# Four chunks of a part worked as one run of high, then low products, in an fp32 decoder trunk on one core

## What is computed

```python
def reference(x, ...):
    h = x
    for i in range(2):
        xn = rms_norm(h, norm_mix[i])
        if i == 0:   # HGRN2: q, f, v, g = split(xn @ w_in (2048 x 8192)); gated recurrence over 16 heads
            mix = hgrn2_mixer(xn, ...)        # ... then rms_norm, * silu(g), @ w_out (2048 x 2048)
        else:        # B, C, h = split(xn @ w_in (2048 x 6144)); (B * conv3(C * h)) @ w_out
            mix = short_conv_mixer(xn, ...)
        h = h + mix
        xn = rms_norm(h, norm_ffn[i])         # gate, val = split(conv3(xn @ w_up (2048 x 11264)))
        h = h + (silu(gate) * val) @ w_down   # w_down: 5632 x 2048
    return rms_norm(h, final_norm)
```

## Time and profile before

| | us |
|---|---|
| median of 3 runs (2368.31 to 2370.46) | 2368.76 |
| the profiled execution's own time | 2369.03 |
| its span, first to last instruction | 2367.2 |
| PE busy | 2339.4 (99%) |
| PE weight loads busy | 2049.0 (87%) |
| DVE busy | 1708.5 (72%) |
| ACT busy | 1043.5 (44%) |
| DMA engines, mean share / rate | some 60% / 184 GB/s |

### The profile page before, as it was taken

The page is one execution under the profiler, slowest core; times in us unless marked ns, Lnnn a source line. Parts: engine busy times, 40 slices in busy tenths (PEclk is TensorE's granted clock), DMA queues, the critical chain, the costliest instruction groups (busy, mean ns, idle before and its releaser), DMA issues.

```text
span 2367.2 us, 36548 instructions
## 1 busy us (share of the span) xinstructions
PE 2339.4 (99%) x13219; PEld 2049.0 (87%) x13219; DVE 1708.5 (72%) x2153; ACT 1043.5 (44%) x1151; POOL 2.7 (0%) x8
## 2 busy tenths in 40 slices
PE   7999999999999999999999999999999999999998
PEld 6888888888888888888888888888888888888886
DVE  6878788878878878865555666667788788785443
ACT  6443434454444444444444444444444444443443
POOL 0000000000000000000000000000000000000000
PEclk9999999999999999999999999999999999999999
DMA  6555555466666665655556656556656666665664
GB/s 197 169 179 160 166 160 164 152 192 188 186 194 185 187 194 179 194 190 187 188 185 192 188 187 187 187 188 186 194 180 192 189 184 188 193 202 185 193 193 144
DMA packets 411833, 434.90 MB, mean 184 GB/s; under 512 B 13344, under 2 KB 387040, under 8 KB 411616
## 3 DMA queue, kind: packets, MB, share of 16 engines
q1 hardware_dynamic: 411264, 432.51, 59.2%
q10 hardware_dynamic: 480, 1.18, 0.1%
HBM read 431.54 MB, written 2.10 MB: 183 GB/s over the span
## 4 chain that ended last, share of the span: by engine, by line
PE 96%; DVE 1%; issue 1%; ACT 1%; DMA 0%; SPq 0%; ACTq 0%; DVEq 0%
PE acc L1050 54%; PE acc L1056 28%; PE acc L1085 3%; PE acc L1086 3%; PE acc L1084 3%; PE acc L1068 2%; PE side L1179 1%; PE acc L1070 1%; PE side L1151 0%; DMA raw<-in_hgrn_w_in 0%; PE side L1174 0%; ACT w_parts L336 0%; DVE kl L788 0%; DVE a_diag L825 0%; DVE a_diag L819 0%
## 5 line engine op out<-in xcount | busy, mean ns | idle before, releaser
L545 DVE TENSOR_TENSOR w_parts<-raw,w_parts 128x1024 fp32r<-128x1024 f32 x816 | 994.4, 1223 | 578.9 <-ACT w_parts L336 569.0
L336 ACT ACTIVATE w_parts<-raw 128x1024 fp32r<-128x1024 f32 x816 | 862.6, 1060 | 1181.4 <-PE acc L1056 975.4
L1050 PE MATMUL acc<-xn,w_parts 128*128 128x512 f32 x4352 | 1094.5, 393 | 3.2 <-DVE xn L604 3.2
L1050 PEld LDWEIGHTS acc<-xn,w_parts 128*128 128x128 f32 x4352 | 783.7, 189 | 144.3 <-DVE xn L604 3.6
L1056 PEld LDWEIGHTS acc<-xn,w_parts 128*128 128x128 f32 x4352 | 594.1, 190 | 42.8
L1056 PE MATMUL acc<-xn,w_parts 128*128 128x256 f32 x4352 | 607.0, 282 | 0.0
L1050 PE MATMUL acc<-act,w_parts 128*128 128x512 f32 x1216 | 305.0, 393 | 1.6 <-DVE act L859 1.6
L1050 PEld LDWEIGHTS acc<-act,w_parts 128*128 128x128 f32 x1216 | 218.7, 189 | 41.0 <-DVE act L859 1.8
L1056 PEld LDWEIGHTS acc<-act,w_parts 128*128 128x128 f32 x1216 | 165.9, 190 | 11.9
L1056 PE MATMUL acc<-act,w_parts 128*128 128x256 f32 x1216 | 169.5, 282 | 0.0
L1084 PE MATMUL acc<-w_parts,act 128*128 128x512 f32 x352 | 137.3, 390 | 0.0
(11 more groups left out here) (131 smaller groups left out, 1005.2 us busy)
## 6 DMA issues: line engine op xcount, KB each, us to landing
raw<-in_ffn_w_up SPq DMA_DIRECT2D x352, 512.0 KB, 4.1
raw<-in_ffn_w_down SPq DMA_DIRECT2D x176, 512.0 KB, 4.3
raw<-in_hgrn_w_in SPq DMA_DIRECT2D x128, 512.0 KB, 3.6
raw<-in_sc_w_in SPq DMA_DIRECT2D x96, 512.0 KB, 4.5
raw<-in_hgrn_w_out SPq DMA_DIRECT2D x32, 512.0 KB, 3.6
raw<-in_sc_w_out SPq DMA_DIRECT2D x32, 512.0 KB, 4.6
x_tok<-in_x SPq DMA_DIRECT2D x4, 512.0 KB, 8.0
out<-h SPq DMA_DIRECT2D x4, 512.0 KB, 4.1
```

The costliest lines, as they stand in the source:

```text
L336: nc.scalar.activation(w_parts[:, c % RING, :, 0, :], raw[:, c % RING], ACT.Copy).then_inc(hi_ready, 1)
L545: v.tensor_tensor(w_parts[:, c % RING, :, 1, :], raw[:, c % RING], w_parts[:, c % RING, :, 0, :].bitcast(F32), ALU.subtract).then_inc(lo_r ...
L1050: mm(to[:, j, :], w[:, q, 0, j * P:(j + 1) * P], src[:, k * KW + q, :, :].rearrange("p n t -> p (n t)"), start=begin and q == 0, stop=Fals ...
```

## The change

A group is worked in runs of chunks: 4 in UP0, UP1, SC_IN and SC_OUT, 2 in HGRN_IN, HGRN_OUT and DOWN0, 1 in DOWN1. PE does the high products (512 columns) of all chunks of a run, then the low products (256 columns) of all of them. `chunk_used` becomes two counts: `hi_used`, raised by the last high product of a chunk, which ACT's `split` waits for, and `lo_used`, raised by its last low product, which DVE's `split` now waits for beside `hi_ready`. In the value group of HGRN_IN the 512-column matmuls (both weight parts moving) of two chunks come first and free the low slots, then the 256-column ones free the high slots. What PE did after chunk kk of a run (stages, turns) now stands after the high products of the run, for the last chunk of the run after its low products. In `PLAN` levels 0 and 2 move one chunk later. The program of DOWN1 is as it was, but for the two counts.

```diff
+RUN = 2
...
-PLAN = [(2, LEVEL, -1), (3, LEVEL, 0), (5, LEVEL, 1), (6, LEVEL, 2), (8, LEVEL, 3), (10, LEVEL, 4),
+PLAN = [(2, LEVEL, -1), (4, LEVEL, 0), (5, LEVEL, 1), (7, LEVEL, 2), (8, LEVEL, 3), (10, LEVEL, 4),
         (12, LEVEL, 5), (13, LEVEL, 6), (15, LEVEL, 7), (18, OUTPUT, 0)]
...
-        chunk_used = sem("chunk_used")
+        hi_used = sem("hi_used")
+        lo_used = sem("lo_used")
...
                 act_e.wait_ge(w_loaded[c % RING], at(i, 4 * phase.cpi, 16 * (c // RING + 1)))
-                act_e.wait_ge(chunk_used, at(i, phase.cpi, c + 1))
+                act_e.wait_ge(hi_used, at(i, phase.cpi, c + 1))
                 nc.scalar.activation(w_parts[:, c % RING, :, 0, :], raw[:, c % RING], ACT.Copy).then_inc(hi_ready, 1)
 
             def correction(i, phase, g, part, c):
 
-                act_e.wait_ge(chunk_used, at(i, phase.cpi, c + 1 + RING))
+                done = hi_used if phase is HGRN_IN and g == V_GROUP else lo_used
+                act_e.wait_ge(done, at(i, phase.cpi, c + 1 + RING))
                 a = g * phase.parts + part
                 act_e.wait_ge(acc_free, at(i, phase.api, phase.a0 + a + SETS))
...
                 dve.wait_ge(hi_ready, at(i, phase.cpi, c + 1))
+                dve.wait_ge(lo_used, at(i, phase.cpi, c + 1))
                 v.tensor_tensor(w_parts[:, c % RING, :, 1, :], raw[:, c % RING],
                                 w_parts[:, c % RING, :, 0, :].bitcast(F32), ALU.subtract).then_inc(lo_ready, 1)
...
-                        dve.wait_ge(chunk_used, at(i, phase.cpi, c + 1 + RING))
+                        dve.wait_ge(lo_used, at(i, phase.cpi, c + 1 + RING))
...
-            def features(to, c, src, k, begin, end, await_low):
+            def feature_highs(to, c, src, k, begin):
 
                 w = w_parts[:, c % RING]
                 for q in range(KW):
                     for j in range(TW):
-
-                        mm(to[:, j, :], w[:, q, 0, j * P:(j + 1) * P],
-                           src[:, k * KW + q, :, :].rearrange("p n t -> p (n t)"), start=begin and q == 0, stop=False,
-                           skip_group_check=True)
-                await_low()
+                        o = mm(to[:, j, :], w[:, q, 0, j * P:(j + 1) * P],
+                               src[:, k * KW + q, :, :].rearrange("p n t -> p (n t)"), start=begin and q == 0,
+                               stop=False, skip_group_check=True)
+                o.then_inc(hi_used, 1)
+            def feature_lows(to, c, src, k, end):
+                w = w_parts[:, c % RING]
                 for q in range(KW):
                     for j in range(TW):
                         o = mm(to[:, j, T:], w[:, q, 1, j * P:(j + 1) * P], src[:, k * KW + q, 0, :], start=False,
                                stop=end and q == KW - 1, skip_group_check=True)
-                return o
-
-            def tokens(to, c, src, k, begin, end, await_low):
+                o.then_inc(lo_used, 1)
+            def x_block(src, t, n, b):
+                return x_mirror[:, t, n] if b else src[:, t, n, 0:P]
+            def token_boths(to, c, src, k, begin):
 
                 w = w_parts[:, c % RING]
-                await_low()
                 for q in range(KW):
-                    t = k * KW + q
                     for b in range(T // P):
-                        x_hi, x_lo = ((x_mirror[:, t, n] if b else src[:, t, n, 0:P]) for n in range(2))
-                        mm(to[:, b, :], x_hi, w[:, q].rearrange("p n d -> p (n d)"), start=begin and q == 0, stop=False,
-                           skip_group_check=True)
-                        o = mm(to[:, b, T:], x_lo, w[:, q, 0, :], start=False, stop=end and q == KW - 1,
-                               skip_group_check=True)
-                return o
-
...
-                        for kk, (part, k, begin, end) in enumerate(phase.steps(first, g)):
-                            c = phase.c0 + g * phase.cpg + kk
-                            a = g * phase.parts + part
-                            if begin:
-
-                                pe.wait_ge(acc_free, at(i, phase.api, phase.a0 + a + 1))
-                            need = k + 1 if phase.parts == 2 else k * KC // TG + 1
-                            if first and g == 0 and need > seen:
-                                pe.wait_ge(ready, ready0 + need * per)
-                                seen = need
-
-                            def await_low():
-                                pe.wait_ge(lo_ready, at(i, phase.cpi, c + 1 + RING))
-
-                            pe.wait_ge(hi_ready, at(i, phase.cpi, c + 1))
-                            work = features
-                            if first and phase is HGRN_IN and g == V_GROUP and part == 0:
-                                pe.wait_ge(mirror_ready, k + 1)
+                        steps = phase.steps(first, g)
+                        run = 1 if phase is DOWN1 else 2 * RUN if phase in (UP0, SC_IN, SC_OUT, UP1) else RUN
+                        for k0 in range(0, phase.cpg, run):
+                            chunks = []
+                            for kk in range(k0, k0 + run):
+                                part, k, begin, end = steps[kk]
+                                c = phase.c0 + g * phase.cpg + kk
+                                a = g * phase.parts + part
+                                if begin:
+                                    pe.wait_ge(acc_free, at(i, phase.api, phase.a0 + a + 1))
+                                need = k + 1 if phase.parts == 2 else k * KC // TG + 1
+                                if first and g == 0 and need > seen:
+                                    pe.wait_ge(ready, ready0 + need * per)
+                                    seen = need
+                                pe.wait_ge(hi_ready, at(i, phase.cpi, c + 1))
+                                to = acc[:, a % SETS]
+                                if phase is DOWN1:
+                                    pe.wait_ge(lo_ready, at(i, phase.cpi, c + 1 + RING))
+                                    wide_tokens(to, c, src, k, begin, end)
+                                elif phase is HGRN_IN and g == V_GROUP:
+                                    if first and part == 0:
+                                        pe.wait_ge(mirror_ready, k + 1)
+                                    pe.wait_ge(lo_ready, at(i, phase.cpi, c + 1 + RING))
+                                    token_boths(to, c, src, k, begin)
+                                else:
+                                    feature_highs(to, c, src, k, begin)
+                                chunks.append((c, to, k, end))
                             if phase is DOWN1:
-                                work = wide_tokens
-                            elif phase is HGRN_IN and g == V_GROUP:
-                                work = tokens
-                            work(acc[:, a % SETS], c, src, k, begin, end, await_low).then_inc(chunk_used, 1)
-                            if carry and first:
-                                carry(g, kk)
-                            if first and rs and (g, kk) == rs_at:
-                                sum_squares(*rs)
-                            if pieces:
-                                pieces(i, first, g, kk)
+                                between(i, first, g, k0)
+                                continue
+                            for kk in range(k0, k0 + run - 1):
+                                between(i, first, g, kk)
+                            for c, to, k, end in chunks:
+                                if phase is HGRN_IN and g == V_GROUP:
+                                    token_highs(to, c, src, k, end)
+                                else:
+                                    pe.wait_ge(lo_ready, at(i, phase.cpi, c + 1 + RING))
+                                    feature_lows(to, c, src, k, end)
+                            between(i, first, g, k0 + run - 1)
...
-            pe.sem_inc(chunk_used, RING)
+            pe.sem_inc(hi_used, RING)
+            pe.sem_inc(lo_used, RING)
```

More of the change, by code:

```diff
@@ L475, in final @@
                 if first and (g, kk) == (0, 0):
-                    act_e.wait_ge(chunk_used, DOWN1.c0 + RING)
+                    act_e.wait_ge(lo_used, DOWN1.c0 + RING)
                     act_e.dma_start(final_w[:], final_norm.partition_broadcast(P)).then_inc(final_w_loaded, 16)
@@ L983, in final @@
                     return
-                dve.wait_ge(chunk_used, DOWN1.c0 + (n + 1) * DOWN1.cpg + RING)
+                dve.wait_ge(hi_used, DOWN1.c0 + (n + 1) * DOWN1.cpg + RING)
                 for b in range(T // P):
@@ L1057, in features, with token_highs, wide_tokens @@
                                stop=end and q == KW - 1, skip_group_check=True)
-                return o
-            def tokens(to, c, src, k, begin, end, await_low):
+                o.then_inc(lo_used, 1)
+            def x_block(src, t, n, b):
```

(39 more changed lines are left out.)

## The result

The changed kernel takes 2424.92 us (median of 4 runs, 2423.79 to 2426.68), the kernel before 2369.59 in the runs beside it: a ratio of 1.0233, 95% interval 1.022 to 1.0246. It is 55 us slower. The forecast was 40 us slower (2409.5, range 2380 to 2432), so the direction and the kind of loss came out, and the size some 15 us short.

What follows compares the result with a forecast made beforehand. PE's matmul stream was taken to bound the kernel. The terms, -9 + 32 + 10 + 4 + 2.5 + 1 = 40.5 us, on the profiled 2369.0 gave 2409.5 us, range 2380 to 2432.

Steps and rivals of the forecast that it cites:

- A: All regrouped phases: fewer turns between high and low products save 9 us, bounds 0 and -12.
- the rival of a full overlap: Long runs let weight loads overlap fully, matmuls fall to columns over 2.4 GHz: -108 us, 2310 in all; chance 4%.
- The rule that the prediction took from the Trainium skill: Matmul gap set by columns alone, 216 ns for 512; order worth nothing, waits stay: 2418 us, chance 12%.
- B: UP0 and UP1: PE waits 1.44 us for the last chunk's high split, 22 times: +32 us, bounds 20 to 42.
- C: HGRN_IN's value group, four iterations: +2.2 us each for level 1, +0.3 for later levels: +10, bounds 2 and 18.
- D: HGRN_OUT's first group: PE's wait for the last tile of `act` grows to 5.9 us: +4, bounds 2 and 6.
- E: Kernel start: less work ahead of the wait for input tile 2, next tile later: +2.5 us, bounds 0.5 and 4.
- F: Other phase starts, where DVE's last work of a phase holds a bank: +1 us, bounds 0 and 3.
- That everything is there in time: UP has no wait, HGRN_IN's value group costs nothing, almost only the regrouping saving counts: 2362 us, chance 6%.
- That the loads get late too: Loads burst behind `lo_used`, making a UP run's last chunk 1.4 us late once more: 31 us, 2440 in all; chance 10%.

Runs made afterwards that it cites:

- experiment 8: Changed kernel with runs of four in UP0, UP1, SC_IN, two in DOWN0, SC_OUT, one elsewhere, SiLU one chunk later, old level places: 2362.32 us.
- Experiment 1: Changed kernel with ACT's SiLU in UP one chunk later, behind the split of chunk 7 instead of ahead of it: 2385.67 us.
- experiment 6: Changed kernel with runs of one in the first group of HGRN_OUT only: 2417.88 us.
- experiment 4: Changed kernel with runs of one in HGRN_IN and the levels where they were before: 2407.77 us.
- experiments 1 and 2: Experiment 1, and the changed kernel with DVE's two convolution steps of UP ahead of the splits, SiLU not moved: 2386.41 us for the latter.
- experiment 3: Changed kernel with runs of two instead of four in UP0 and UP1, SiLU not moved: 2386.77 us.
- experiment 7: Changed kernel with runs of one in every phase and the levels where they were before: 2368.9 us.

## Why the prediction was right in kind and short in size

**A, regrouping saves 9 us: right.** With runs of four and nothing waiting, an iteration of UP loses 44.69 - 44.45 = 0.24 us for 12 pairs of turns, 0.020 each (0.018 in the prediction); with runs of two, 0.16 for 8, the same 0.020. DOWN0 loses 0.88 for 44. SC_IN gave 0.9 where 72 turns should give 1.4: ten of its twelve groups took 22.23 us instead of 22.35, which is the full saving, but the first took 23.50 instead of 23.21 and the second 22.34, with a wait of 0.25 us for a bank. In a run of 32 of the changed kernel the steps stay at 0.227 but for the first five (0.228 to 0.236), so the rival of a full overlap falls. The rule that the prediction took from the Trainium skill (TensorE: Matmul & The Clock Gate, "Back-to-back issue gap"), by which the gap follows from the columns alone, doesn't hold to this precision: the order moved 6.3 us in experiment 8, and a run of 512 columns keeps 227 ns, not its 216. The Trainium skill calls that, in the same section, the gap of isolated matmuls, and for a stream of weight loads and matmuls it gives some 131 ns at 512 columns; no row here comes near that either.

**B, the split of the last chunk late in UP: right, 15% too small.** Predicted 1.44 us a time and 32 in all; measured 1.54 in UP1, some 1.65 in UP0. Small things were left out: DVE's split starts some 0.1 us after the low product's end, not 0.04, PE starts 0.06 after the split of the last chunk has ended, and behind a wait the first high product takes 0.34 us instead of 0.23. Per iteration the loss is 46.12 - 44.45 = 1.67 in UP1 and 46.24 - 44.45 = 1.79 in UP0. Experiment 1 against the change puts both phases together at 37.4 us. The 0.1 that UP0 waits longer lies in DVE's first convolution step: from L630 to L632 it takes 0.88 us there and 0.75 in UP1. Why is left open.

**C, the value group: the wait was right, the rest mis-sized.** Predicted: a wait of 2.4 at level 1, +2.2 an iteration net, and +0.3 for all later levels; in all 10. The timeline of PE in the changed kernel, answering to the earlier trace rows:

```profile
91.24 1.54 PE L1214 MATMUL side<-ql,kl 128*128 128x128 f32 x8 [2.01 <-DVE kl L792]
92.43 0.77 PE L1076 MATMUL acc<-w_parts,xn 128*128 128x512 f32 x1
93.00 0.63 PE L1076 MATMUL acc<-w_parts,x_mirror 128*128 128x512 f32 x1
93.42 0.63 PE L1076 MATMUL acc<-w_parts,xn 128*128 128x512 f32 x1
...
95.44 0.40 PE L1076 MATMUL acc<-w_parts,x_mirror 128*128 128x512 f32 x1
```

The wait is 2.0 to 2.2, and the wait of 0.6 at level 2 of the earlier trace rows is gone, so the net cost of level 1 was less than the 2.2 forecast: where the clock stayed up (experiment 1, second iteration) the value group took 28.95 us, 1.2 more than before. But the wide products behind the wait start 0.43 us apart here instead of 0.23, and the stretches of this trace say why (PE busy, weight loads, DVE, ACT, POOL, then the granted clock as a share of full speed):

```profile
92.43:95.40 2.97, 2.97 (x9) 2.38 (x9) 2.97 (x4) 0.00 (x0) 0.00 (x0) 0.52 0.31 74
95.50:99.00 3.50, 3.50 (x23) 3.14 (x22) 2.37 (x5) 0.30 (x1) 0.00 (x0) 1.00 0.75 230
```

For some 3 us TensorE's granted clock is at about half, the 1.2 GHz level, and then back at 2.4 GHz. Some 7 products start 0.2 us late each; by the value groups of experiment 1 it costs 1.6 us a time, and it isn't in the sum. And the later levels cost 1.4 us an iteration, not 0.3: group 3 went from 26.78 to 28.19, with waits of 0.4 and 1.0 us for the keys. So C is 4 x (2.75 + 1.41) = 16.6 instead of 10.

**D, HGRN_OUT: the wait was right, its follow-up missing.** Predicted wait 5.9 us, measured 6.0. But the granted clock behind it is 0.50 until 474.15, which isn't in the sum:

```profile
468.30:471.80 3.50, 3.50 (x8) 2.75 (x9) 0.00 (x0) 0.00 (x0) 0.00 (x0) 0.50 0.25 85
```

The 8 high products took 1.7 us more (3.78 against 2.11 in experiment 6), and with the low ones behind them the half clock cost some 2.7 us in this execution. The phase lost 6.8 us, 7.2 without the 0.3 that A gives it, instead of 4.

**E, the start: not settled.** The first group took 32.3 us against 30.9. But over the executions of all the kernels here it was 30.4 to 33.2 with runs of one (four of them) and 31.9 to 33.0 with runs of two (six), so the start varies as much from one execution to the next as E was said to cost. The clock goes with it: from 17.8 to 35 us the granted clock is 1.00 in the two quickest, the kernel before (30.9) and experiment 4 (30.4), and 0.80 to 0.90 in the other eight.

**F, the other phase starts: too small.** Measured against what A gives, SC_OUT lost 1.6, SC_IN 0.5 and each UP phase 0.5 (the first iteration of experiment 1, 45.83 - 44.45, against 45.55 - 44.69 before): 3.1 instead of 1, just above the upper bound. SC_OUT's loss is a wait of 1.0 us for DVE and its restart, and it is gone with the runs of two of experiment 8.

**The sum, term by term.** E here is the one pair of traces, and may be chance.

| | A | B | C | D | E | F | sum |
|---|---|---|---|---|---|---|---|
| predicted | -9 | 32 | 10 | 4 | 2.5 | 1 | 40.5 |
| measured | -9.0 | 37.4 | 16.6 | 7.2 | 1.4 | 3.1 | 56.7 |

The 16 us that the sum missed are 5 in B, 7 in C, 3 in D and 2 in F, less 1 in E. In C and D the half clock, 4 x 1.6 + 2.7 = 9 us, stood in no term; the later levels were 4.4 too small, and level 1 was 4 too large, which hid a part of it.

**The rivals.** That everything is there in time would have given 2362, and experiment 8, where it is made so, gives 2362.3. That the two agree so closely is partly luck: experiment 8 regroups less (6.3 us, not A's 9), and has HGRN_OUT's 1.0 besides. That the loads get late too: ACT's splits do wait for loads in the change (372 us in all), but in experiments 1 and 2 they wait as long and PE doesn't.

## What to carry to other kernels

When work is regrouped so that a buffer comes free later, count from the new time of freeing through everything that stands behind the waiting instruction on its engine, on to the next engine, and compare with the new time of need: here 0.24 us saved an iteration stood against a chain that was 1.5 us late, and one instruction moved by one place made up for it. Run length is a dose: two chunks gave two thirds of the saving with 4 us to spare, four took all of the margin. And a wait put into a matmul stream can cost more than its length: here the granted clock stayed up behind waits of 1.5 us, and fell behind most of those of 2.0 us.

## What the runs showed of the hardware that I had not expected

The clock behind a wait. After the 22 waits in UP, in which PE stood idle for 0.9 to 1.7 us, the granted clock stays at 1.00; before the change, the waits of 0.6 at level 2 show no slow products either. After the wait of 6.0 us in HGRN_OUT it is at 0.50, in all six traces that have this wait. After the waits of 2.0 to 2.2 us in the value group it fell in each of the four iterations of the change, but not always in others: over the five traces with this wait, 18 times of 20. The two exceptions are the second iteration of experiment 1 and the first of experiment 3 (value group 28.93 us). A stretch behind a wait in UP of the change:

```profile
1749.00:1752.00 3.00, 3.00 (x17) 2.66 (x18) 1.80 (x2) 2.50 (x4) 0.00 (x0) 1.00 0.62 190
```

Two stretches of experiment 1, behind the wait of the second and of the third iteration:

```profile
198.40:201.40 3.00, 3.00 (x17) 2.53 (x16) 3.00 (x4) 0.00 (x0) 0.00 (x0) 1.00 0.16 40
303.50:306.50 3.00, 3.00 (x9) 2.35 (x8) 3.00 (x4) 0.00 (x0) 0.00 (x0) 0.50 0.32 93
```

The value group took 28.95 us there in the second iteration and 30.53 in the third. This is the half clock measured by itself in one execution: 1.58 us. Why it fell the one time and not the other, no run here tells. DVE was busy all through both stretches, PE stood idle 2.0 us ahead of either, as these rows of the same trace show:

```profile
197.73 1.15 PE L1214 MATMUL side<-ql,kl 128*128 128x128 f32 x8 [2.02 <-DVE kl L792]
198.63 0.48 PE L1076 MATMUL acc<-w_parts,xn 128*128 128x512 f32 x1
198.95 0.39 PE L1076 MATMUL acc<-w_parts,x_mirror 128*128 128x512 f32 x1
...
302.18 1.15 PE L1214 MATMUL side<-ql,kl 128*128 128x128 f32 x8 [2.01 <-DVE kl L792]
303.08 0.60 PE L1076 MATMUL acc<-w_parts,xn 128*128 128x512 f32 x1
303.48 0.63 PE L1076 MATMUL acc<-w_parts,x_mirror 128*128 128x512 f32 x1
```

Length alone doesn't decide it. At the start the kernel before waits 2.76 us and its 8 high products then take 2.11 us, at full clock; in experiment 7 the same place has 2.90 us, and they take 3.78:

```profile
28.59 3.78 PE L1053 MATMUL acc<-xn,w_parts 128*128 128x512 f32 x8 [2.90 <-DVE xn L608]
```
